# Spare TensorE products at stage ends and layer heads, and the last square summed from its own buffer

## The reference, cut to what matters

```
def _layer(x, past, prm):
    h = _rmsnorm(x, g)
    p = _split_cols(jnp.einsum('nld,dc->nlc', h, w_in))
    ...
    mix = jnp.concatenate([ret_o * silu(p['ret_g']), sb_o * silu(p['sb_g']),
                           dsa_o * silu(p['dsa_g']), rw_o * silu(p['rw_g'])], axis=-1)
    x = x + jnp.einsum('nlc,cd->nld', mix, w_out)
...
y_prompt = _rmsnorm(hp, final_g)
y_sample = _rmsnorm(hs, final_g)
```

## Time and profile before

| | |
|---|---|
| median of three executions | 2989.84 us (2989.01 to 2990.37) |
| the profiled execution's own time | 2991.68 us |
| its span, first to last instruction | 2989.9 us |
| mean granted TensorE clock over the span | 0.956 |
| TensorE busy | 2745.0 us, 92% |
| VectorE busy | 1489.3 us, 50% |
| ScalarE busy | 917.3 us, 31% |

### The profile page before, as it was taken

How to read it: one execution, slowest core, us unless ns; L and a number is a source line. 1 busy time by engine, 2 the same in 40 slices (tenths; PEclk the granted TensorE clock), 3 DMA queues, 4 the chain that set the end, 5 groups by cost and what they waited for, 6 DMA issues and landing times. The chain is left out here.

```text
span 2989.9 us, 61239 instructions
## 1 busy us (share of the span) xinstructions
PE 2745.0 (92%) x25414; PEld 2536.1 (85%) x25414; DVE 1489.3 (50%) x2604; ACT 917.3 (31%) x1742; POOL 149.0 (5%) x301
## 2 busy tenths in 40 slices
PE   5998999999899997989979989999989999888997
PEld 5997988897787987879979889889877688787997
DVE  4332253336745585963343323532477267589433
ACT  3222253223222342232232223432322215422322
POOL 2100000000011000000002000000000200000001
PEclk7999999999999899989989999999999989998999
DMA  5322334632233222034333233265322422300543
GB/s 177 93 73 73 79 108 113 204 108 72 50 93 86 55 65 88 3 108 136 107 80 91 55 91 97 79 193 155 90 55 54 110 57 76 99 16 13 155 136 126
DMA packets 398474, 277.98 MB, mean 93 GB/s; under 512 B 34460, under 2 KB 368332, under 8 KB 394606
## 3 DMA queue, kind: packets, MB, share of 16 engines
q1 hardware_dynamic: 397278, 263.50, 31.7%
q10 hardware_dynamic: 912, 10.50, 0.9%
HBM read 237.75 MB, written 36.18 MB: 92 GB/s over the span
## 5 line engine op out<-in xcount | busy, mean ns | idle before, releaser
L320 PE MATMUL acc<-h_hi,in_w_hi 128*128 128x272 f32 x3968 | 897.5, 308 | 63.3 <-DVE h_lo L652 35.6
L320 PE MATMUL acc<-h_lo,in_w_hi 128*128 128x272 f32 x3968 | 831.1, 291 | 0.0
L320 PE MATMUL acc<-h_hi,in_w_lo 128*128 128x272 f32 x3968 | 830.1, 291 | 0.0
L320 PEld LDWEIGHTS acc<-h_hi,in_w_hi 128*128 128x128 f32 x3968 | 637.1, 192 | 148.2 <-issue 69.9
L320 PEld LDWEIGHTS acc<-h_lo,in_w_hi 128*128 128x128 f32 x3968 | 635.6, 192 | 0.0
L320 PEld LDWEIGHTS acc<-h_hi,in_w_lo 128*128 128x128 f32 x3968 | 632.0, 192 | 0.0
L350 DVE TENSOR_TENSOR in_w_lo<-in_w_raw,in_w_hi 128x512 fp32r<-128x512 f32 x496 | 346.0, 704 | 422.3 <-ACT in_w_hi L346 419.6
L346 ACT CAST in_w_hi<-in_w_raw 128x512 fp32r<-128x512 f32 x496 | 303.3, 617 | 398.8 <-PE acc L320 311.0
L320 PE MATMUL dr_bank<-over_both,out_weights 128*128 128x272 f32 x1984 | 280.3, 288 | 1.7 <-DVE over_both L691 1.7
L320 PEld LDWEIGHTS dr_bank<-over_both,out_weights 128*128 128x128 f32 x1984 | 260.8, 188 | 1.9 <-DVE over_both L691 1.9
L350 DVE TENSOR_TENSOR out_weights<-regions,out_weights 128x512 fp32r<-128x512 f32 x128 | 88.3, 692 | 182.8 <-ACT out_weights L346 182.7
(11 more groups left out here) (407 smaller groups left out, 3284.2 us busy)
## 6 DMA issues: line engine op xcount, KB each, us to landing
in_w_raw<-in_w_in SPq DMA_DIRECT2D x488, 256.0 KB, 2.9
region<-in_cache_sb_kv SPq DMA_DIRECT2D x128, 256.0 KB, 3.1
regions<-in_w_out SPq DMA_DIRECT2D x128, 256.0 KB, 2.8
regions<-in_cache_dsa SPq DMA_DIRECT2D x64, 160.0 KB, 2.2
region<-x_spill SPq DMA_DIRECT2D x32, 272.0 KB, 3.6
x_spill<-region SPq DMA_DIRECT2D x32, 272.0 KB, 2.1
mix_spill<-mix SPq DMA_DIRECT2D x6, 1088.0 KB, 5.5
mix_back<-mix_spill SPq DMA_DIRECT2D x6, 1088.0 KB, 8.6
```

Of the source, the lines that this page charges most:

```text
L320: last = pe.matmul(self.place(i)[:, c, 0:HALF_N], w[:, u % RING, t, :], part[f][:, HALF_N * c:HALF_N * c + HALF_N], start=first and w is k ...
```

## The change

A new helper `keep_busy` issues `n` products of the identity with 240 columns of the constant table, in fp32, into the unused columns 272 to 511 of a PSUM bank. Nobody reads them. They are placed

- after the last sum of `begin`: 4;
- at the head of a layer: 8 at once, 4 more when four tiles are normed, 1 more when four tiles are rounded, and then the projections start;
- at the end of a layer's projections (the end of `front`), once the second-last tile is kept: 5;
- at the end of a layer: 1 between the keeping of tile 14 and of tile 15, and 3 after the sums.

The last square (tile 15) is no longer added to `total` by VectorE. TensorE sums over `total`, which has squares 0 to 14, and over the buffer of the last square, with two more products of ones that accumulate in the same bank. It waits for tile 15 to be kept before it starts the first pair.

More of the change, by code:

```diff
@@ L180, in wait, with keep_busy @@
         self.engine.wait_ge(self.sem, self.n)
+def keep_busy(pe, k, bank, n):
+    for _ in range(n):
+        pe.matmul(bank[:, HALF_N:512], k.c("ident"), k.table[:, 0:512 - HALF_N], start=True, stop=True)
 def inverse_root(act, logged, x, scale=1.0, at=0):
```

## The result

Twelve executions of the changed kernel have a median of 2983.13 us, twelve of the kernel before, beside them, 2990.11 us. The ratio is 0.9977 with a 95% interval of 0.9969 to 0.9984: 7.0 us faster, where 3.9 was forecast and the range went down to 2982.6. One comparison isn't all that there is. The same kernel was timed again in the study (run `after_again`): 0.9988, interval 0.9979 to 0.9997, that is 3.8 us by the medians (2986.48 against 2990.24). Its 24 executions together have a mean of 2984.9 us, the 103 of the kernel before that were made in the study 2990.1: 5.2 us, with a standard error of about 0.9. So the change is worth some 5 us, and single executions of it lie between 2976.4 and 2995.4.

A forecast was written before the change was run, and what follows sets the result against it. TensorE, busy for 92% of the span, was taken to bound the kernel. Gains of 1.5 + 0.4 + 1.6 + 0.4 = 3.9 us took 2989.84 to 2985.9 us, with a range of 2982.6 to 2989.6.

The forecast's parts named there:

- more than the sum: Rival, chance 0.19: later clock rises move forward or the delta rule starts warm; two such effects give 2982.7 us.
- Start of the kernel, cost 0: First stage: 4 spare products may delay the next stage 1.6 us, but `prm` waits behind `x_spill`; bounds 0 and 1.6.
- a sign of being wrong: Start of layer 0: the prediction would be wrong if `prm` landed later; first norm was to stay at 50.5 us.
- What one spare product costs: All places: one 240-column fp32 product on TensorE takes 0.4 us at full clock, 0.8 us at half clock.
- Head of layer 0, 1.5 us: Start of layer 0's projections: clock rises earlier, near 58.4 us; 1.5 us gained, bounds 2.2 gained and 0.2 lost.
- Head of layer 1, 1.6 us: Start of layer 1's projections: whole half-clock stretch saved; 1.6 us gained, bounds 2.0 gained and 0.8 lost.
- Layer ends, 0.4 each: End of each layer: summing the last square straight from its buffer ends the sums 0.4 us earlier.
- End of the projections, 0: Before the delta rule: 5 spare products cost and gain 0, leaving 3.8 us idle; warm start up to 1.7 us a layer.
- The last stage, not in the sum: From the transposes back to token rows until the end: the forecast had only the layer end ahead of it.
- Given back later: Rival, chance 0.16: between head and layer end, earlier starts only add half-clock work, halving the gain each time; 2988.5 us.
- Don't raise the clock: Rival, chance 0.07: spare products leave the clock at half and only stand in the way; 2991.6 us, slower.
- Hidden anyway: Rival, chance 0.10: VectorE's chain sets the layer heads, so only the layer ends count; 2989.0 us.

The follow-up runs named there:

- the third row of the table above: Four follow-up kernels without full spare products at the heads: half clock for 2.9 to 3.8 us after the first projection, heads 22.8 to 23.2 us.
- e1_heads_only: Kernel before plus only the 8, 4 and 1 spare products at each layer head; 2985.15 us, ratio 0.9981.
- e6_front_ten: Changed kernel with 10 in place of 5 spare products after the projections; 2976.82 us, ratio 0.9956 (5 executions).
- e9_ten_only: Kernel before plus only 10 spare products after the projections; 2985.17 us, ratio 0.9991.
- e3_square_only: Kernel before plus only TensorE's own sum over the last square, no spare product anywhere; 2989.76 us, ratio 0.9998.
- e7_end_spares: Changed kernel plus 4 spare products in the last stage, after the first 16 transposes; 2986.83 us, ratio 0.9987.
- e4_thin_heads: Changed kernel with the heads' spare products cut from 240 to 8 columns, same places and waits; 2989.82 us, ratio 0.9998.

## Why the prediction was right

It forecast faster by 3.9 us, most likely within 0.2% of no change; two comparisons gave 7.0 and 3.8 us, together 5.2. The direction, the places and their order were right; the first comparison lies where the rival "more than the sum" was put, which had a chance of 0.19. But in the profile neither of that rival's two ways is what happened: the delta rule started at half clock in both layers, and the stretch between head and layer end gave 0.3 us at most. So that the time lies so near the end of the range is in part luck, as the terms show one by one.

*Start of the kernel, cost 0.* Right, and for the reason given. The stage was held back by 1.5 us, against the bound of 1.6, and `prm` landed when `x_spill` did. By the letter `prm` landed 0.2 us later, which I had named as a sign of being wrong. But those 0.2 us aren't the spare products' doing: `x_spill` was itself issued 0.4 us later, ahead of all of them, and its issue lies anywhere from 35.7 to 38.9 us over the fourteen profiles. From that issue to the landing of `prm` it is 13.1 to 13.2 us in the nine profiles with these four products and 13.4 in the five without.

*What one spare product costs.* 16 records in 3.48 us at full clock are 0.43 us a product, and 13 in 5.20 us at half clock 0.80 us. Taken were 0.4 and 0.8.

*Head of layer 0, 1.5 us.* The steps came as written: the clock fell behind the first 8, the next four started at 53.6, the last spare product ended at 57.5 (57.4). The rise came at 57.0 in place of 58.4, and TensorE's 1.7 us became enough to meet VectorE's bound: 2.2 us by the length of the head, 2.05 by the table's lead, which has the 0.2 us of the start in it. The term was too small by 0.5 to 0.7. One reading of the rows failed: I had taken 5.1 and 4.9 us from restart to rise for fixed. Here the rise came 3.3 us after the restart at 53.6, and in four other kernels without full spare products at the heads it comes 2.9 to 3.8 us after the first projection. *Head of layer 1, 1.6 us:* 1.9 measured, against a cap of 2.0. The clock wasn't lost in the waits around the last spare product. In both heads VectorE's own work is the limit now.

How much of that is the kernel before's bad luck? Its profiled execution has the two latest rises of all and 23.8 us in both heads. The four kernels in the third row of the table above have a mean of 23.0, and the heads with all 13 spare products one of 21.8. So by the profiles the usual gain is 1.2 us a head rather than 2.0, and the forecast of 3.1 for both heads was too high for the usual execution and too low for the one profiled. By the timings the heads are worth more: leaving them out or thinning them cost 2.4 us (2987.3 against 2984.9) and 4.5 us of mean time, with standard errors of about 1.5, and the heads alone (`e1_heads_only`) gave 5.4 us by the means, with one of about 1.1. What gives the rest isn't shown.

*Layer ends, 0.4 each.* 0.36 measured in the two profiles, by the working given: the second pair of sums starts 1.11 us after the first (1.1), which is why the add's 0.72 don't all arrive.

*End of the projections, 0.* Right: the idle time of 3.84 us was to be 3.8, the delta rule started at half clock, and without the 5 nothing changed. Its bound, up to 1.7 us a layer for a warm start, was right too: 1.6 in `e6_front_ten` against the kernel before.

*The last stage, not in the sum.* In the profiles it is the largest part of what I missed: 2.3 us. It isn't the change's doing, as far as the runs show: the stage took 21.1 us in `e1_heads_only` and in `e9_ten_only`, which have no spare product there, 23.8 in `e3_square_only` and 22.6 in `e7_end_spares`, which has the most. It goes with how long `gain_rows` takes to land (4.3 to 6.1 us), with where the clock stands behind the wait for it (10.6 us from there to the last output's issue, or 11.9 to 12.9), and with how long the last output takes to land (3.8 to 5.8 us).

*Given back later.* It didn't happen in the profile: the lead of 2.05 us at the head of layer 0 was 1.97 at its last gate. In layer 1 the lead fell from 4.6 to 3.8 us at that gate, but it was 5.0 at the root, which is the 4.6 and the layer end's 0.4. But the thing that this rival and its opposite describe is there. From the last `h_lo` to the root, the stretch takes 1418.7 to 1426.3 us over the profiles of the kernels without the ten (with them from 1417.7), whose programs there differ only by the spare products after the projections and the last sums. `after_again` had 1426.3 and 1424.1 us, the changed kernel's first profile 1423.0 and 1423.4. The stretch goes with the clock: over the 28 layers of the fourteen profiles TensorE is busy at half clock for 65 to 82 us of it, and a line through the points rises by 0.43 us per us (correlation 0.85). The shortest, 1417.7 us in `e6_front_ten`, has 65.4 us of such work, and the longest, in `after_again`, 81.9, where the changed kernel's first profile had 73.1. That is a correlation and not an experiment. The Trainium skill (TensorE: Matmul & The Clock Gate, Part 1) has the gate's timing run free of the kernel, which would make such a scatter; the runs show the scatter, but no run sets when the clock falls, so the cause isn't isolated.

Of the 4.3 us between the spans of the changed kernel's two profiles, 1.3 had arisen before `x_spill` was issued and 4.0 in these stretches, and 1.0 was won back between the root of layer 0 and the first `h_lo` of layer 1. Whether the same makes up the difference of 7.0 and 3.8 us between the two comparisons can't be said, since each of them has one profile.

*The other rivals.* "Don't raise the clock" is refuted by the windows of both heads; `e4_thin_heads` shows what it would have looked like. "Hidden anyway" is refuted by VectorE's timeline, in which the wait of 2.25 us is gone.

The best version that the study found is the changed kernel with 10 in place of 5 spare products after the projections: 0.9956 and 0.9968 in its two comparisons, 11 executions of 2974.3 to 2985.3 us.

## What to carry to other kernels

Where TensorE restarts after a wait, look at its clock in windows on both sides and price the stretch at half clock; then ask which engine would be the next bound once it is gone, since that caps the gain (2.0 us here, not 2.3). Look at more than one execution: the restarts of the profiled one were at half clock for 5 us, those of four other kernels for 3 to 4. Spare products have to reach up to the restart: here 5 in a wait of 5.9 us bought nothing, 10 bought 1.6 us each time. A product at a stage's end can hold up the barrier, here by 1.5 us; that cost nothing because the first thing of the next stage waited for the DMA behind `x_spill`.

## What the runs showed of the hardware that I had not expected

The clock stayed full through idle times of 1.82 us in all four kernels with ten (eight delta-rule starts), and it was at half behind the idle times of 3.84 and 5.87 us in every kernel that had them there (in some of those, L2551's first 32 products took 3.3 us in place of 3.6, between the two levels).

A DMA of 1024 KB at the same place of the program landed between 4.3 and 6.1 us after its issue, over fourteen profiles, and one of 256 KB, the last output, between 3.8 and 5.8 us.

Executions of one program, on one core of each of several chips, spread over 12.5 us (0.4%) in the kernel before, 2983.7 to 2996.2, and over 19 us in the changed one, 2976.4 to 2995.4, so that differences of 0.1% need more than the 12 executions that one comparison has.
